# Another order of the VectorE and ScalarE work in the first two chunks of each feed-forward layer

## The chip, the cores and the metric

The kernel runs on one core of a Trainium2 chip. The metric is the device time of one execution in microseconds (us); less is better. The program is written engine by engine: TensorE (PE), VectorE (DVE), ScalarE (ACT), GpSimd (POOL) and the DMA queue of SyncE (SP) each have an instruction list of their own that runs strictly in its order, and semaphores tie the lists together.

## The reference

The input x has 256 tokens of 1024 numbers. Seven stages follow: a hybrid mixer, a feed-forward layer, a convolution block, a second feed-forward layer, a third one that opens the second block, a retention and pooling stage, and a fourth feed-forward layer, with a last norm. The change touches the four feed-forward layers alone. Each is (with a weight of 1 or 0.5 on the last sum)

```python
def swiglu(h, wg, wu, wd):
    return (jax.nn.silu(h @ wg) * (h @ wu)) @ wd

h = h + weight * swiglu(rms_norm(h, gain), wg, wu, wd)      # wg, wu: 1024 x 2816, wd: 2816 x 1024, all float32
```

## The kernel before, in words

**Split products.** Every float32 matmul is three matmuls on rounded parts: an operand is a high part (`whi`, `xh`, `yh`), which ScalarE makes with a rounding copy, and a low part (`wlo`, `xl`, `yl`), which VectorE makes as the value less the high part. `mm3` issues high x high, high x low and low x high (L256, L257, L258).

**Weights as units.** All weights stream through as units of 128 x 2048 numbers (1 MB). There are four raw buffers and four split buffers. `hi(v)` (ACT, L210) waits for unit v to have landed and for the matmuls that used unit v-4 (`used`); `lo(v)` (DVE, L217) waits for `hi(v)`. `hi_half` (ACT, L251) does it in two halves and `lo_quarter` (DVE, L241) in four quarters. SP loads unit v once `lo(v-4)` is done.

**A feed-forward layer** is cut into 11 chunks of 256 hidden columns (j = 0 to 10). Chunk j reads two input units: `quarter` is 12 matmuls (4 k-blocks x 3) of one token half t and one unit, and four quarters make the gate and up columns of the chunk in a PSUM bank per token half. Then

- `scalar_gate_ffn(j, t)` (ACT, L527) takes silu of the gate columns into `sil`,
- `vector_gate_ffn(j, t)` (DVE, L633) multiplies it by the up columns into `hid` and frees the bank. In the layers of weight 0.5 a tiny instruction (L627) scales the norm first, for j = 0,
- `tensor_hidden(j)` (PE, L264) transposes `hid`, both token halves, with four small matmuls.

For chunks 0 to 7 (`FAST` = 8) the product with the down unit is one step of a fast 2 x 2 block scheme with seven products in place of eight. It needs sums of blocks on both sides:

- the activations: `scalar_turned` (ACT) copies the transposed chunk into `turned` (L545) and rounds three of its blocks (L552, signal `turned_hi`); `vector_turned` (DVE, L646) makes their low part; GpSimd forms four sums (L793 to L798); `scalar_sums` (ACT, L556) rounds them, and `vector_sums` (DVE, L651) makes their low part (`sums_lo`),
- the weights: `vector_mix` (DVE, L664 to L670, four instructions) forms the sums of the down unit, one of them in place in the raw buffer, which `hi_half` of that unit must wait for; `scalar_mixed` (ACT, L562) rounds three of them and `vector_mixed` (DVE, L675) makes their low part (`mixed_lo`).

`tensor_fast(j, products)` (PE) issues the named products, three matmuls each. Products 0, 1 and 3 use blocks of `turned`; 2, 4, 5 and 6 use the sums. Products 3, 5 and 6 also need `mixed_lo`.

**Units of a layer.** u0 and u0+1 are the input of chunk 0, u0+2 and u0+3 of chunk 1, u0+4 the down unit of chunk 0, u0+5 and u0+6 the input of chunk 2, u0+7 the down unit of chunk 1.

**PE's order in chunk 1:** quarter (u0+2, t=0); `tensor_hidden(0)`; quarter (u0+3, t=0); products 0 and 1 of chunk 0; quarter (u0+2, t=1), which goes into bank 7 like the t=0 part and so waits for `vector_gate_ffn(1, 0)` to free it; quarter (u0+3, t=1); products 2 and 3; `tensor_hidden(1)`; products 4, 5 and 6. Chunks 2 to 8 repeat this.

**DVE's order in chunks 0 and 1 before:** low parts of the normed activations of t=1 (L361), `lo(u0+3)`, mix 0, gate (0,0), `lo(u0+4)`, gate (0,1), `lo(u0+5)`, turned 0, sums 0, gate (1,0), mixed 0, mix 1, quarters 0 and 1 of u0+6, gate (1,1), quarters 2 and 3 of u0+6.

**ACT's order before:** norm of t=1 (L344, L353), `hi(u0+3)`, gate (0,0), both halves of u0+4, gate (0,1), `hi(u0+5)`, turned 0, sums 0, mixed 0, gate (1,0), `hi(u0+6)`, gate (1,1), first half of u0+7, turned 1, second half of u0+7.

Of the kernel before, what the change touches and what calls it, by code (L numbers as in the profile page):

```python
# [9 lines left out]
FAST = 8  # L10
# [119 lines left out]
def build(nc, xin, wst, wg, wg2, cst, par, brow, cosin, rmask, pmat, dft, w_dw, b_dw, out):  # L130
    NU = wst.shape[0]
    assert NU == sum(UNITS.values())
    with ExitStack() as ctx:
# [3 lines left out]
        sig = Signals(nc, ctx)  # L137
# [95 lines left out]
            if k == n - 1:  # L233
                sig.alias("lo", (v,), "lo_piece", (v, k))

        def lo_quarter(e, q, v, k):
            q.wait_ge(*sig.at("hi", v))
            if v >= S:
                q.wait_ge(*sig.at("used", v - S))
            cols = slice(UC // 4 * k, UC // 4 * k + UC // 4)  # L240
            e.tensor_tensor(wlo[:, v % S, cols], raw[:, v % R, cols], whi[:, v % S, cols].bitcast(F32),  # L241
                            ALU.subtract).then_inc(*sig.up("lo", v) if k == 3 else sig.up("lo_quarter", v, k))
# [58 lines left out]
        def x_of(name):  # L301
            return lambda t, j: banks.emptied("x", name, t, j)
# [172 lines left out]
        def tensor_ffn(e, q, f):  # L475
            units, weight, before, following, _ = FF[f]
            u0 = U[units]
            x = x_of(f)
            for j in range(FC):
                u, key = ff_in(u0, j), f"{f}_in{j}"  # L480
                fast = 1 <= j <= FAST
                d = ff_down(u0, j - 1)
                quarter(e, q, key, u, 0, 0, in_bank(j, 0), xh, xl, x)
                if j == 0:
                    for half in range(2):
                        turn_x(e, q, f, before, 1, half)
                elif j == 1 or j > FAST + 1:
                    tensor_hidden(e, q, f, j - 1)
                quarter(e, q, key, u, 0, 1, in_bank(j, 0), xh, xl, x)
                if fast:  # L490
                    tensor_fast(e, q, f, d, j - 1, (0, 1))
                if f == "ffn0" and j == FC - 1:
                    tensor_prepare(e, q, 0)
                quarter(e, q, key, u, 1, 0, in_bank(j, 1), xh, xl, x)
                if f == "ffn0" and j == FC - 1:
                    tensor_prepare(e, q, 1)
                quarter(e, q, key, u, 1, 1, in_bank(j, 1), xh, xl, x)
                if f == "ffn0" and j == FC - 1:
                    tensor_prepare(e, q, 2)
                if fast:  # L500
                    tensor_fast(e, q, f, d, j - 1, (2, 3))
                    tensor_hidden(e, q, f, j)
                    tensor_fast(e, q, f, d, j - 1, (4, 5, 6))
            sig.alias("x_free", (f,), "full5", (f"{f}_in{FC - 1}", 1))
            u = [ff_down(u0, j) for j in range(FAST, FC)]
            for t in range(2):
                q.wait_ge(*sig.at("yl", f, FAST))
                out_part(e, q, f, u[0], t, 2 * (FAST % 4), yh, yl, ACC[t], first=True)
                if t == 0:
                    tensor_hidden(e, q, f, FC - 1)  # L510
            for n in range(1, 3):
                q.wait_ge(*sig.at("yl", f, FAST + n))
                out_part(e, q, f, u[n], 0, 2 * ((FAST + n) % 4), yh, yl, ACC[0], last=n == 2)
            out_part(e, q, f, u[1], 1, 2 * ((FAST + 1) % 4), yh, yl, ACC[1])
            if following:
                for half in range(2):
                    turn_x(e, q, following, f, 0, half)
            out_part(e, q, f, u[2], 1, 2 * ((FAST + 2) % 4), yh, yl, ACC[1], last=True)
            sig.alias("y_free", (f,), "full3", ("acc", f, 1, 1))
# [44 lines left out]
        def scalar_ffn(e, q, f):  # L564
            units, weight, before, following, _ = FF[f]
            u0 = U[units]
            norm_act(e, q, f, before, 1)
            hi(e, q, u0 + 3)
            scalar_gate_ffn(e, q, f, 0, 0)
            hi_half(e, q, u0 + 4, 0)  # L570
            hi_half(e, q, u0 + 4, 1)
            scalar_gate_ffn(e, q, f, 0, 1)
            hi(e, q, u0 + 5)
            for j in range(1, FAST + 1):
                d = ff_down(u0, j - 1)
                if j == 1:
                    scalar_turned(e, q, f, 0)
                scalar_sums(e, q, f, j - 1)
                if j > 1:
                    hi(e, q, d + 1)  # L580
                scalar_mixed(e, q, f, j - 1)
                scalar_gate_ffn(e, q, f, j, 0)
                hi(e, q, d + 2)
                scalar_gate_ffn(e, q, f, j, 1)
                hi_half(e, q, d + 3, 0)
                if j < FAST:
                    scalar_turned(e, q, f, j)
                else:
                    scalar_hidden(e, q, f, j)
                hi_half(e, q, d + 3, 1)  # L590
            q.wait_ge(*banks.filled("fast", f, 0))
            q.wait_ge(*sig.at("mixed_lo", ff_down(u0, FAST - 1)))
            e.activation(fastw[0], ps[FAST_BANK[0]][:, :], ACT.Copy, bias=0.0, scale=1.0).then_inc(*banks.empty("fast", f, 0))
            hi(e, q, u0 + 29)
            scalar_gate_ffn(e, q, f, FC - 2, 0)
            if f == "ffn0":
                scalar_taps(e, q)
            hi(e, q, u0 + 30)
            scalar_gate_ffn(e, q, f, FC - 2, 1)
            hi(e, q, u0 + 31)  # L600
            scalar_hidden(e, q, f, FC - 2)
            scalar_gate_ffn(e, q, f, FC - 1, 0)
            if f == "ffn0":
                scalar_waves(e, q)
                scalar_prepare(e, q, 0)
            hi(e, q, u0 + 32)
            if f == "ffn0":
                scalar_prepare(e, q, 1)
            scalar_gate_ffn(e, q, f, FC - 1, 1)
            if f == "ffn0":  # L610
                scalar_prepare(e, q, 2)
            hi(e, q, u0 + 33)
            scalar_hidden(e, q, f, FC - 1)
            hi(e, q, u0 + 34)
            if following:
                norm_act(e, q, following, f, 0, sig.at("x_free", f))
            hi(e, q, u0 + 35)
# [112 lines left out]
        def vector_ffn(e, q, f):  # L730
            units, weight, before, following, _ = FF[f]
            u0 = U[units]
            norm_dve(e, q, f, 1)
            lo(e, q, u0 + 3)
            vector_mix(e, q, f, 0)
            vector_gate_ffn(e, q, f, 0, 0)
            lo(e, q, u0 + 4)
            vector_gate_ffn(e, q, f, 0, 1)
            lo(e, q, u0 + 5)
            for j in range(1, FAST + 1):  # L740
                d = ff_down(u0, j - 1)
                if j > 1:
                    lo(e, q, d)
                vector_turned(e, q, f, j - 1)
                vector_sums(e, q, f, j - 1)
                if j > 1:
                    lo(e, q, d + 1)
                vector_gate_ffn(e, q, f, j, 0)
                vector_mixed(e, q, f, j - 1)
                if j < FAST:  # L750
                    vector_mix(e, q, f, j)
                lo_quarter(e, q, d + 2, 0)
                lo_quarter(e, q, d + 2, 1)
                vector_gate_ffn(e, q, f, j, 1)
                lo_quarter(e, q, d + 2, 2)
                lo_quarter(e, q, d + 2, 3)
            vector_hidden(e, q, f, FAST)
            vector_combine(e, q, f, (0,))
            lo(e, q, u0 + 28)
            vector_combine(e, q, f, (1,))  # L760
            vector_gate_ffn(e, q, f, FC - 2, 0)
            lo(e, q, u0 + 29)
            vector_combine(e, q, f, (2,))
            vector_gate_ffn(e, q, f, FC - 2, 1)
            if f == "ffn0":
                vector_taps(e, q)
            lo(e, q, u0 + 30)
            vector_hidden(e, q, f, FC - 2)
            vector_gate_ffn(e, q, f, FC - 1, 0)
            lo(e, q, u0 + 31)  # L770
            if f == "ffn0":
                vector_waves(e, q)
            lo(e, q, u0 + 32)
            vector_gate_ffn(e, q, f, FC - 1, 1)
            lo(e, q, u0 + 33)
            vector_hidden(e, q, f, FC - 1)
            lo(e, q, u0 + 34)
            residual(e, q, f, before, 0, ACC[0], combined=f)
            if following:
                norm_dve(e, q, following, 0)  # L780
            residual(e, q, f, before, 1, ACC[1], combined=f)
            lo(e, q, u0 + 35)
# [1828 lines left out]
```

## Time and profile before

| | |
|---|---|
| median of 3 runs | 1248.78 us (1247.76 to 1249.49) |
| the profiled execution | 1248.3 us |
| its span, first to last instruction | 1246.5 us |
| mean granted TensorE clock | 0.992 of full speed |
| busy: PE, DVE, ACT, POOL | 1207.1, 911.2, 673.1, 100.6 us |
| load of a unit (1 MB), median from issue to landing | 4.8 us |
| starts of the four feed-forward layers (first matmuls of the turned x of t=1) | 149.5, 430.4, 617.0 and 1055.0 us |

All times in rows are from the start of the span. A row of a timeline has a start, a length, the engine, the line, the operation, and out<-in; instructions of one kind that follow each other are merged into one row with their count. What stands in brackets is the time that the engine was idle before it and what released it. An engine's neighbouring instructions overlap by some hundredths of a us at their ends.

### The profile page before, as it was taken

To read this page: it belongs to the slowest core of one execution; us is meant where nothing else is said; L and a number is where in the kernel's file an instruction comes from. 1 tells how busy PE (TensorE), PEld (TensorE's weight loads), DVE (VectorE), ACT (ScalarE), POOL (GpSimd) and SP (SyncE) were. 2 spreads that over 40 slices of the span, in tenths; PEclk is the share of its full clock that TensorE was granted. 3 is DMA by queue.
4 is the path that set the end of the run, shared out by engine and by line. 5 is a ranking of instruction groups with operands and counts; after the bars stand their busy time and mean duration, and the time that the engine had idled before them with its cause. 6 is when DMAs were issued, how large, how long until landed. Compare 5 with 4: busy or idle time off the path is not lost.

```text
span 1246.5 us, 14254 instructions
## 1 busy us (share of the span) xinstructions
PE 1207.1 (97%) x5534; PEld 986.8 (79%) x5534; DVE 911.2 (73%) x1124; ACT 673.1 (54%) x810; POOL 100.6 (8%) x171
## 2 busy tenths in 40 slices
PE   7999999999998989999989999999999999899997
PEld 5776878888887868888878888888888878688885
DVE  6556788888669688887688887656477665788883
ACT  6454656655645656654556654555434544665551
POOL 2300011110020011110011110000000000111100
PEclk9999999999999999999999999999999999999999
DMA  9422455555640545555545555745553444455540
GB/s 344 149 101 80 157 210 189 188 197 203 216 173 34 203 162 189 192 200 180 192 165 188 191 198 179 285 178 180 186 199 135 155 183 156 157 195 202 186 168 34
DMA packets 32326, 220.71 MB, mean 177 GB/s; under 512 B 3729, under 2 KB 4129, under 8 KB 6530
## 3 DMA queue, kind: packets, MB, share of 16 engines
q1 hardware_dynamic: 32258, 219.79, 48.9%
q8 instruction: 44, 0.72, 0.2%
q14 instruction: 24, 0.20, 0.0%
HBM read 218.72 MB, written 1.05 MB: 176 GB/s over the span
## 4 chain that ended last, share of the span: by engine, by line
PE 88%; ACT 4%; DVE 4%; issue 2%; POOL 1%; DMA 0%; SPq 0%; POOLq 0%; DVEq 0%; ACTq 0%
PE ps L256 28%; PE ps L258 27%; PE ps L257 27%; PE ps L261 3%; PE ps L264 3%; DVE wlo L217 1%; ACT xh L344 1%; ACT whi L210 1%; POOL st L377 0%; ACT FS L562 0%; ACT AR L353 0%; ACT whi L251 0%; POOL sums L793 0%; DVE hid L633 0%; DMA pr<-in_par 0%
## 5 line engine op out<-in xcount | busy, mean ns | idle before, releaser
L217 DVE TENSOR_TENSOR wlo<-raw,whi 128x2048 fp32r<-128x2048 f32 x166 | 387.7, 2336 | 154.0 <-ACT whi L210 104.6
L256 PE MATMUL ps<-whi,xh 128*128 128x512 f32 x1120 | 445.7, 398 | 10.1 <-DVE hid L633 6.0
L257 PE MATMUL ps<-wlo,xh 128*128 128x512 f32 x1120 | 439.0, 392 | 0.0
L258 PE MATMUL ps<-whi,xl 128*128 128x512 f32 x1120 | 439.0, 392 | 0.0
L210 ACT CAST whi<-raw 128x2048 fp32r<-128x2048 f32 x163 | 311.7, 1913 | 204.6 <-PE ps L258 203.8
L256 PEld LDWEIGHTS ps<-whi,xh 128*128 128x128 f32 x1120 | 211.8, 189 | 61.0 <-DVE hid L633 7.7
L258 PEld LDWEIGHTS ps<-whi,xl 128*128 128x128 f32 x1120 | 212.0, 189 | 45.9
L257 PEld LDWEIGHTS ps<-wlo,xh 128*128 128x128 f32 x1120 | 212.3, 190 | 41.7
L256 PE MATMUL ps<-whi,yh 128*128 128x512 f32 x352 | 142.5, 405 | 0.9 <-DVE yl L1655 0.6
L258 PE MATMUL ps<-whi,yl 128*128 128x512 f32 x352 | 138.1, 392 | 0.0
L257 PE MATMUL ps<-wlo,yh 128*128 128x512 f32 x352 | 138.0, 392 | 0.0
L241 DVE TENSOR_TENSOR wlo<-raw,whi 128x512 fp32r<-128x512 f32 x132 | 85.1, 686 | 27.2 <-ACT whi L210 27.1
L527 ACT ACTIVATE sil<-ps,st 128x256 f32<-128x256 f32 x88 | 41.9, 476 | 84.1 <-PE ps L258 84.1
L377 POOL TENSOR_TENSOR st<-st,nhalf 128x1 f32<-128x1 f32 (+3 forms) x28 | 28.1, 1002 | 705.6 <-DVE st L368 402.2
L251 ACT CAST whi<-raw 128x1024 fp32r<-128x1024 f32 x72 | 74.8, 1044 | 12.0 <-DVE raw L666 10.1
L256 PEld LDWEIGHTS ps<-whi,yh 128*128 128x128 f32 x352 | 66.7, 189 | 14.8 <-DVE yl L1655 1.0
L258 PEld LDWEIGHTS ps<-whi,yl 128*128 128x128 f32 x352 | 66.6, 189 | 14.2
L257 PEld LDWEIGHTS ps<-wlo,yh 128*128 128x128 f32 x352 | 66.8, 190 | 12.2
L344 ACT ACTIVATE xh<-ps,pr 128x128 fp32r<-128x128 f32 x112 | 30.5, 382 | 51.6 <-PE ps L264 48.3
L675 DVE TENSOR_TENSOR FS<-AR,FS 128x1536 fp32r<-128x1536 f32 x32 | 55.9, 1748 | 0.0
L633 DVE SCALAR_TENSOR_TENSOR hid<-ps,st,sil 128x256 f32<-128x256 f32 x88 | 42.5, 483 | 18.0 <-ACT sil L527 15.4
L793 POOL TENSOR_TENSOR sums<-AR 128x128 f32<-128x128 f32 x32 | 17.0, 530 | 432.6 <-ACT AR L545 432.6
(215 smaller groups left out, 1127.5 us busy)
## 6 DMA issues: line engine op xcount, KB each, us to landing
raw<-in_w SPq DMA_DIRECT2D x199, 1024.0 KB, 4.8
raw<-in_w SPq DMA_DIRECT2D x4, 256.0 KB, 4.9
raw<-in_w SPq DMA_DIRECT2D x2, 512.0 KB, 6.9
AR<-in_b_pw SPq DMA_DIRECT2D x1, 1024.0 KB, 4.8
AR<-in_gate_bias SPq DMA_DIRECT2D x1, 1024.0 KB, 8.5
out<-AR SPq DMA_DIRECT2D x2, 512.0 KB, 2.6
AR<-in_dft SPq DMA_DIRECT2D x1, 864.0 KB, 7.6
AR<-in_rmask SPq DMA_DIRECT2D x1, 768.0 KB, 10.1
```

The source lines that it names most:

```text
L210: e.copy(whi[:, v % S, :], raw[:, v % R, :]).then_inc(*sig.up("hi", v))
L217: e.tensor_tensor(wlo[:, v % S, :], raw[:, v % R, :], whi[:, v % S, :].bitcast(F32), ALU.subtract).then_inc(*sig.up("lo", v))
L241: e.tensor_tensor(wlo[:, v % S, cols], raw[:, v % R, cols], whi[:, v % S, cols].bitcast(F32), ALU.subtract).then_inc(*sig.up("lo", v) if k ...
L251: e.copy(whi[:, v % S, cols], raw[:, v % R, cols]).then_inc(*sig.up("hi", v) if k else sig.up("hi_half", v))
L256: e.matmul(o, ah, bh, start=start, stop=False, skip_group_check=skip)
L257: e.matmul(o, ah, bl, start=False, stop=False, skip_group_check=skip)
L258: return e.matmul(o, al, bh, start=False, stop=stop, skip_group_check=skip)
L261: return e.matmul(o, a, b, start=start, stop=stop, skip_group_check=skip)
L344: last = e.activation(xh[:, k, tcols(t)], ps[b][:, 128 * i:128 * i + 128], ACT.Copy, bias=0.0, scale=parm(name, k))
L527: e.activation(sil[:, t, :], ps[banks.of[key, t]][:, 0:256], ACT.Silu, bias=0.0, scale=rstd[:, t:t + 1]).then_inc(*sig.up("sil", f, j, t))
L633: e.scalar_tensor_tensor(out=hid[:, t, :], in0=ps[b][:, 256:512], scalar=scale, in1=sil[:, t, :], op0=ALU.mult, op1=ALU.mult).then_inc(*ba ...
L675: e.tensor_tensor(mixl, mix, mixh.bitcast(F32), ALU.subtract).then_inc(*sig.up("mixed_lo", v))
```

## The change

In chunks 0 and 1 of every feed-forward layer:

- DVE: mix 0 goes in front of `lo(u0+3)`; gate (0,1) goes in front of the split of u0+4; that of u0+4 and u0+5 is made in quarters, the first two of u0+4 as soon as its first half is rounded; turned 0 and gate (1,0) go between quarters 1 and 2 of u0+5; mixed 0 and mix 1 go in front of sums 0; u0+6 is split whole, behind gate (1,1).
- ACT: gate (0,1) goes in front of the halves of u0+4; gate (1,0) and then mixed 0 go in front of sums 0.
- PE: in all chunks 1 to 8, product 3 is issued in front of product 2.

```diff
-        def lo_quarter(e, q, v, k):
-            q.wait_ge(*sig.at("hi", v))
+        def lo_quarter(e, q, v, k, ready="hi"):
+            q.wait_ge(*sig.at(ready, v))
...
                 if fast:
-                    tensor_fast(e, q, f, d, j - 1, (2, 3))
+                    tensor_fast(e, q, f, d, j - 1, (3, 2))
                     tensor_hidden(e, q, f, j)
                     tensor_fast(e, q, f, d, j - 1, (4, 5, 6))
...
             norm_act(e, q, f, before, 1)
             hi(e, q, u0 + 3)
             scalar_gate_ffn(e, q, f, 0, 0)
+            scalar_gate_ffn(e, q, f, 0, 1)
             hi_half(e, q, u0 + 4, 0)
             hi_half(e, q, u0 + 4, 1)
-            scalar_gate_ffn(e, q, f, 0, 1)
             hi(e, q, u0 + 5)
+            scalar_turned(e, q, f, 0)
             for j in range(1, FAST + 1):
                 d = ff_down(u0, j - 1)
                 if j == 1:
-                    scalar_turned(e, q, f, 0)
-                scalar_sums(e, q, f, j - 1)
-                if j > 1:
+                    scalar_gate_ffn(e, q, f, 1, 0)
+                    scalar_mixed(e, q, f, 0)
+                    scalar_sums(e, q, f, 0)
+                else:
+                    scalar_sums(e, q, f, j - 1)
                     hi(e, q, d + 1)
-                scalar_mixed(e, q, f, j - 1)
-                scalar_gate_ffn(e, q, f, j, 0)
+                    scalar_mixed(e, q, f, j - 1)
+                    scalar_gate_ffn(e, q, f, j, 0)
                 hi(e, q, d + 2)
...
             norm_dve(e, q, f, 1)
+            vector_mix(e, q, f, 0)
             lo(e, q, u0 + 3)
-            vector_mix(e, q, f, 0)
             vector_gate_ffn(e, q, f, 0, 0)
-            lo(e, q, u0 + 4)
             vector_gate_ffn(e, q, f, 0, 1)
-            lo(e, q, u0 + 5)
-            for j in range(1, FAST + 1):
+            for k in range(4):
+                lo_quarter(e, q, u0 + 4, k, "hi_half" if k < 2 else "hi")
+            lo_quarter(e, q, u0 + 5, 0)
+            lo_quarter(e, q, u0 + 5, 1)
+            vector_turned(e, q, f, 0)
+            vector_gate_ffn(e, q, f, 1, 0)
+            lo_quarter(e, q, u0 + 5, 2)
+            lo_quarter(e, q, u0 + 5, 3)
+            vector_mixed(e, q, f, 0)
+            vector_mix(e, q, f, 1)
+            vector_sums(e, q, f, 0)
+            vector_gate_ffn(e, q, f, 1, 1)
+            lo(e, q, u0 + 6)
+            for j in range(2, FAST + 1):
                 d = ff_down(u0, j - 1)
-                if j > 1:
-                    lo(e, q, d)
+                lo(e, q, d)
                 vector_turned(e, q, f, j - 1)
                 vector_sums(e, q, f, j - 1)
-                if j > 1:
-                    lo(e, q, d + 1)
+                lo(e, q, d + 1)
                 vector_gate_ffn(e, q, f, j, 0)
                 vector_mixed(e, q, f, j - 1)
```

## Rows read from the trace of the kernel before

**Rows 1.** Waits of PE: line, releaser, us in total, times, longest.

```profile
PE ps L264 <- DVE hid L633: 9.6, 4, 2.5
```

**Rows 2.** Timeline of PE, first feed-forward layer, chunks 0 to 2.

```profile
158.17 0.39 PE L258 MATMUL ps<-whi,xl 128*128 128x512 f32 x1
...
160.89 0.39 PE L258 MATMUL ps<-whi,xl 128*128 128x512 f32 x1
163.56 0.63 PE L264 MATMUL ps<-kc,hid 128*128 128x128 f32 x4 [2.28 <-DVE hid L633]
...
170.58 0.50 PE L256 MATMUL ps<-whi,xh 128*128 128x512 f32 x1 [0.70 <-DVE hid L633]
...
177.52 0.60 PE L264 MATMUL ps<-kc,hid 128*128 128x128 f32 x4
...
180.02 0.39 PE L256 MATMUL ps<-whi,xh 128*128 128x512 f32 x1
```

**Rows 3.** Timeline of PE, same places of the second and the fourth feed-forward layer.

```profile
444.48 0.62 PE L264 MATMUL ps<-kc,hid 128*128 128x128 f32 x4 [2.28 <-DVE hid L633]
451.51 0.50 PE L256 MATMUL ps<-whi,xh 128*128 128x512 f32 x1 [2.28 <-DVE hid L633]
...
1069.24 0.63 PE L264 MATMUL ps<-kc,hid 128*128 128x128 f32 x4 [2.50 <-DVE hid L633]
1076.28 0.50 PE L256 MATMUL ps<-whi,xh 128*128 128x512 f32 x1 [2.31 <-DVE hid L633]
```

**Rows 4.** Timeline of DVE, first feed-forward layer, chunks 0 to 2.

```profile
154.99 2.29 DVE L217 TENSOR_TENSOR wlo<-raw,whi 128x2048 fp32r<-128x2048 f32 x1 [1.65 <-ACT whi L210]
157.20 0.68 DVE L664 TENSOR_TENSOR AR<-raw 128x512 f32<-128x512 f32 x1
...
160.73 2.29 DVE L217 TENSOR_TENSOR wlo<-raw,whi 128x2048 fp32r<-128x2048 f32 x1 [0.26 <-ACT whi L251]
162.94 0.48 DVE L633 SCALAR_TENSOR_TENSOR hid<-ps,st,sil 128x256 f32<-128x256 f32 x1
...
165.53 0.81 DVE L646 TENSOR_TENSOR yl<-AR,yh 128x384 fp32r<-128x384 f32 x1
...
170.44 1.75 DVE L675 TENSOR_TENSOR FS<-AR,FS 128x1536 fp32r<-128x1536 f32 x1
...
175.64 1.29 DVE L241 TENSOR_TENSOR wlo<-raw,whi 128x512 fp32r<-128x512 f32 x2 [0.47 <-ACT whi L210]
...
182.75 0.55 DVE L646 TENSOR_TENSOR yl<-AR,yh 128x384 fp32r<-128x384 f32 x1
```

**Rows 5.** Timeline of ACT, first feed-forward layer, chunks 0 and 1.

```profile
154.81 0.53 ACT L527 ACTIVATE sil<-ps,st 128x256 f32<-128x256 f32 x1
158.69 2.00 ACT L251 CAST whi<-raw 128x1024 fp32r<-128x1024 f32 x2 [3.36 <-DVE raw L666]
...
160.96 1.89 ACT L210 CAST whi<-raw 128x2048 fp32r<-128x2048 f32 x1
164.22 0.60 ACT L545 ACTIVATE AR<-ps 128x512 f32<-128x512 f32 x1 [1.38 <-PE ps L264]
164.85 0.51 ACT L552 CAST yh<-AR 128x384 fp32r<-128x384 f32 x1
...
168.17 1.48 ACT L562 CAST FS<-AR 128x1536 fp32r<-128x1536 f32 x1
```

**Rows 6.** Timeline of POOL, first feed-forward layer, chunks 0 and 1.

```profile
164.90 1.03 POOL L793 TENSOR_TENSOR sums<-AR 128x128 f32<-128x128 f32 x1 [10.91 <-ACT AR L545]
...
178.83 0.46 POOL L793 TENSOR_TENSOR sums<-AR 128x128 f32<-128x128 f32 x1 [11.22 <-ACT AR L545]
```

**Rows 7.** Windows: stretch, length, busy us (instructions) of each engine, granted clock, DMA share, GB/s.

```profile
163.56:167.62 4.06, 4.06 (x13) 3.28 (x14) 2.78 (x2) 1.11 (x2) 2.63 (x4) 0.58 0.80 295
...
444.40:448.60 4.20, 4.12 (x20) 3.50 (x21) 2.87 (x2) 1.14 (x3) 2.64 (x4) 1.00 0.84 289
```

**Rows 8.** Timeline of SP's queue: the load that follows the split of unit u0.

```profile
133.62 0.33 SPq L2341 DMA_DIRECT2D raw<-in_w  x1
```

## Prediction

> **What bounds the kernel now.** I read the waits of PE first, then the timelines of the engines from the start of the first feed-forward layer, and then the same places of the other three. PE waits rarely, and the largest wait is one of the four feed-forward layers: the transpose of `hid` waits for the gate on VectorE, 9.6 us in four waits [rows 1]. In the first layer PE could go on at 160.89 + 0.23 = 161.12 (12 matmuls take 160.89 - 158.17 = 2.72, so 0.227 each) and goes on at 163.56, 2.44 later. It is held again before quarter (u0+2, t=1), until 170.58, by gate (1,0), which must free bank 7 [rows 2]. From 180.02 on, chunk 2, it runs without a wait. So the reader is to see one stretch per layer, 161.12 to 180.02, 18.90 us long.
>
> What would it take without waits? The transposes cost 2.50 (177.52 to 180.02) less nine matmuls, 0.46 [rows 2]. In the stretch stand 2 x 0.46, 12 + 6 + 24 + 6 = 48 matmuls (10.90) and the last nine (2.04): 13.86. So 5.0 us are there to be had in a layer, and no more.
>
> The half clock is no part of it. In the first layer the granted clock was 0.58 for 4.06 us after the first wait, that is partly 1.2 and partly 2.4 GHz; in the second it was 1.00 in the same place [rows 7]. Yet from the first release to the second took 7.02 us in the one and 7.03 in the other [rows 2, 3]: a chain over ACT, POOL, ACT and DVE sets the second release, and a PE that got there sooner only waited longer (2.28 against 0.70).
>
> **Why the first wait is there.** Gate (0,1) could start when chunk 0 is done: 158.17 + 0.39 = 158.56 and a silu of 0.5 [rows 2, 5]. But ACT first rounds both halves of u0+4, which wait for mix 0 (idle 3.36), and DVE makes `lo(u0+4)`, 160.73 to 163.02, ahead of the gate [rows 4, 5].
>
> **The change, walked through in the first layer.**
>
> DVE: it was idle for 1.65 before `lo(u0+3)`, so from 153.34 [rows 4]. Mix 0 goes there: four instructions of 0.69 and 0.04 between them, 2.9, to 156.24. `lo(u0+3)`, 2.29, ends at 158.53, 1.2 later than before (157.28); PE needs it at 161.6. Gate (0,0) to 158.95.
>
> ACT: silu (0,1) 158.60 to 159.1. Gate (0,1) on DVE ends at 159.6, and PE wants it at 161.12. The first wait goes, with a margin of 1.5.
>
> ACT then makes the halves of u0+4 (2.00, to 161.0) and `hi(u0+5)` (1.89, to 162.8) [rows 5]. The transposes end at about 161.8, so turned 0 is now late by ACT's own queue: 162.8, rounding done 0.6 + 0.5 later, 163.9. This is the new tight place.
>
> DVE meanwhile: u0+4 in quarters, pairs of 1.29 [rows 4], 160.05 to 162.6; quarters 0 and 1 of u0+5, 162.8 to 164.1; turned 0 behind them, 0.55 if undisturbed (second row of its kind), done 164.6. POOL's sums now run beside this. Before, POOL's first sum took 1.03 beside DVE's work and 0.46 without, and turned 0 took 0.81 beside POOL's and 0.55 without [rows 4, 6]. I charge 0.27 twice, for the quarter and for turned 0, as that row is the nearest thing: 165.15. The ends are nothing (164.6) and a whole slow POOL sum of 1.03 (165.65).
>
> The Trainium skill ("SBUF — State Buffer", "Who interferes with whom") says that a VectorE instruction with two inputs in SBUF and a GpSimd instruction that reads SBUF exclude each other, the later one waiting for the end of the earlier. The two rows just named agree with it, and by it VectorE and GpSimd would take turns here, which is the second rival below; the sum does not need it.
>
> PE: 161.12 + 0.46 + 2.72 = 164.30 at products 0 and 1; it waits until 165.15 and its first matmul after a wait is 0.1 longer (0.50 against 0.39, [rows 2]). Six matmuls, 1.36: 166.6. Gate (1,0): its bank is full at 164.5, silu to 164.95, DVE behind turned 0 to 165.6. Bank 7 is free 1.0 before PE asks: the second wait goes. 24 matmuls, 5.45: 172.05.
>
> What is late next: product 3 needs `mixed_lo`. ACT's rounding (1.48, from 164.95) ends at 166.4, DVE after quarters 2 and 3 of u0+5 (167.1) gives it at 168.8. Fine. Mix 1 (2.9) to 171.7, sums 0 (0.69) to 172.4. Product 2 comes at 172.05 + 0.68 = 172.73. In the old order it would come at 172.05 and wait 0.35; that is all that the swap is worth, in chunk 1 alone; in later chunks PE waited for neither, and it costs nothing there. Rounding of the sums on ACT: POOL ends between 165.3 and 167.5 (four of 0.46 to 1.03 from 163.4), so it is done by 168.1 at the latest, before DVE's 171.7. Gate (1,1): silu to 172.7, gate to 173.2; the transposes come at 172.05 + 1.36 = 173.4. As tight as before, but free. `lo(u0+6)`, now whole, ends at 175.5; PE needs it at 178.6.
>
> Chunk 2 then starts at 173.4 + 2.50 = 175.9 in place of 180.02: **4.1 us gained**. It goes on as before, every queue in the same place relative to PE.
>
> Loads: that of u0+4 was issued at 133.6 [rows 8]; at the table's median of 4.8 to landing it is there 15 us before mix 0 wants it. That of u0+7 goes out 1.2 later, 158.6, and is wanted by mix 1 at 168.8. SP's list is not reordered.
>
> The second layer has the same waits to 0.01. In the fourth (and the third, which repeats it) the first wait is 2.50 in place of 2.28, for the small scaling in front of gate (0,1) [rows 3]; the margin of 1.5 covers that, so 4.3. Sum: 2 x 4.1 + 2 x 4.3 = 16.8. The profiled execution took 1248.3; less 16.8 it is 1231.5. The median of the runs is 0.5 above it: **1232.0 us**.
>
> **Rivals.**
>
> 1. POOL and DVE hardly disturb each other: 4.6 a layer, 18.8 in all, 1230; with no wait at all 5.0 and 5.2, 1228.4. Against it: the one place where both ran together shows both lengthened [rows 4, 6]. Chance 0.10.
>
> 2. VectorE becomes the bound. Its work from 153.34 to the end of gate (1,1) adds up to about 17.9 us, to 171.2, against 173.2 in the walk; there is little room. If each instruction beside POOL pays, turned 0 is at 165.65 and sums 0 at 173.0, later than product 2: 0.7 less in a layer, 14.0 in all, 1234.8. Chance 0.14.
>
> 3. The clock falls. The stretch is now PE's own, so a half clock would cost: 4.06 x (1 - 0.58) = 1.7 a layer [rows 7]; in two layers 1235.4, in four 1238.8. Against it: the wait left is 0.85, and the clock fell only after waits of over 2.2, and not after each of them. Chance 0.08.
>
> 4. The other side: mix 0 now heads DVE's list and waits for the load of u0+4 and for the last product of the stage before. Were it held, `lo(u0+3)` and both gates would stand behind it. Up to 1.5 late costs nothing, then 1 for 1 in each layer; 1.5 + 4.1 = 5.6 late, so mix 0 at 159, takes back the whole, and at 6.3 the kernel is slower, about 1251.5. The load would have to take 25 us. Chance 0.03.
>
> 5. The freed time is given back later, by a load or a split that only just came in time: no change, 1248.5. Against it: PE waited for nothing from chunk 2 on, and DVE and ACT hang on PE there and come earlier with it; only loads could lag, and the table's 4.8 us stands against a chunk of some 16. Chance 0.03.
>
> The walk as it stands (1230.5 to 1233.8): 0.62.
>
> **Range.** A change of under 0.2% (2.5 us) can't be told from none. Faster by more: 0.94; within: 0.03; slower: 0.03. The range takes in rival 1 at one end and rivals 2 and most of 3 at the other: 1228.5 to 1237.
>
> **What would show it.** The waits of PE for the gate before the transposes are gone from all four layers, and the wait for bank 7 with them; in their place stands one of 0.4 to 1.4 on turned 0 (L646) before products 0 and 1. Gate (0,1) starts about 2 us ahead of the transposes. Product 2 does not wait. From the first transpose of a layer's `hid` to chunk 2 it is 14.8, where it was 16.5 (163.56 to 180.02), and the transpose comes 2.4 sooner. Wrong I would be if mix 0 starts later than 155, if the clock is under 1 behind the transposes, or if sums 0 ends behind product 3.

## The result and the profile after

The changed kernel takes 1239.53 us, median of 4 runs (1238.23 to 1240.40); the kernel before took 1248.27 beside it (1247.73 to 1249.49). The ratio is 0.9928, interval 0.9911 to 0.9945: faster by 0.7%, 8.7 us. Forecast were 1232.0 us (1228.5 to 1237) and a gain of 16.8. The direction was right; the size was half, and the time lies outside the range.

The profiled execution took 1238.23 us, its span is 1236.4, so 10.1 us shorter than that of before. First PE in the first feed-forward layer (timeline of PE, changed kernel). The lines of PE and ACT have the numbers of before; in the changed kernel the gate on VectorE is L636, turned 0 L649, sums L654, and the sums on POOL L805 to L810, and in runs that add or drop lines above them POOL's are a few off again.

```profile
161.56 0.60 PE L264 MATMUL ps<-kc,hid 128*128 128x128 f32 x4
...
165.67 0.47 PE L256 MATMUL ps<-whi,yh 128*128 128x512 f32 x1 [0.74 <-DVE yl L649]
...
172.59 0.39 PE L256 MATMUL ps<-FS,yh 128*128 128x512 f32 x1
...
173.95 0.60 PE L264 MATMUL ps<-kc,hid 128*128 128x128 f32 x4
...
176.47 0.39 PE L256 MATMUL ps<-whi,xh 128*128 128x512 f32 x1
...
184.85 0.50 PE L256 MATMUL ps<-whi,xh 128*128 128x512 f32 x1 [1.41 <-DVE hid L636]
...
191.79 0.60 PE L264 MATMUL ps<-kc,hid 128*128 128x128 f32 x4
```

PE gets to the transposes 0.4 later than in the trace of before (161.56 and 161.12), for reasons ahead of them. The wait before the transposes [rows 1, 2] is gone, and so is the one for bank 7 in chunk 1. The only wait up to chunk 2 is 0.74 on turned 0. From the first transposes to chunk 2 it is 176.47 - 161.56 = 14.91 (forecast 14.8). But then, in chunk 2, a wait of 1.41 stands at 184.85 that was not there before: again bank 7, again the gate. From the transposes of chunk 1 to those of chunk 2 it takes 191.79 - 173.95 = 17.84. Before, these stood at 177.52 [rows 2] and 193.67, 16.15 apart. Waits of PE over the whole kernel, and the same places of the fourth layer:

```profile
PE ps L256 <- DVE hid L636: 5.7, 4, 1.4
...
PE ps L256 <- DVE yl L649: 3.0, 4, 0.8
...
1063.21 0.47 PE L256 MATMUL ps<-whi,yh 128*128 128x512 f32 x1 [0.76 <-DVE yl L649]
...
1082.37 0.50 PE L256 MATMUL ps<-whi,xh 128*128 128x512 f32 x1 [1.42 <-DVE hid L636]
```

Every layer does the same. Who makes gate (2,0) late? DVE, POOL and ACT of the changed kernel, from the end of chunk 1 on:

```profile
171.99 0.69 DVE L654 TENSOR_TENSOR yl<-sums,yh 128x512 fp32r<-128x512 f32 x1
173.29 0.48 DVE L636 SCALAR_TENSOR_TENSOR hid<-ps,st,sil 128x256 f32<-128x256 f32 x1 [0.61 <-ACT sil L527]
173.69 2.28 DVE L217 TENSOR_TENSOR wlo<-raw,whi 128x2048 fp32r<-128x2048 f32 x1
176.71 2.57 DVE L217 TENSOR_TENSOR wlo<-raw,whi 128x2048 fp32r<-128x2048 f32 x1 [0.74 <-ACT whi L251]
...
182.11 2.29 DVE L217 TENSOR_TENSOR wlo<-raw,whi 128x2048 fp32r<-128x2048 f32 x1 [1.12 <-ACT whi L210]
184.32 0.48 DVE L636 SCALAR_TENSOR_TENSOR hid<-ps,st,sil 128x256 f32<-128x256 f32 x1
```

```profile
175.26 1.04 POOL L805 TENSOR_TENSOR sums<-AR 128x128 f32<-128x128 f32 x1 [8.38 <-ACT AR L545]
...
176.68 0.46 POOL L808 TENSOR_TENSOR sums<-sums,AR 128x128 f32<-128x128 f32 x1
177.22 2.39 POOL L810 TENSOR_TENSOR sums<-AR,sums 128x128 f32<-128x128 f32 x1
```

```profile
179.64 0.62 ACT L556 CAST yh<-sums 128x512 fp32r<-128x512 f32 x1 [2.96 <-POOL sums L810]
180.17 1.91 ACT L210 CAST whi<-raw 128x2048 fp32r<-128x2048 f32 x1
181.98 1.47 ACT L562 CAST FS<-AR 128x1536 fp32r<-128x1536 f32 x1
183.36 0.46 ACT L527 ACTIVATE sil<-ps,st 128x256 f32<-128x256 f32 x1
```

Read it from POOL. Its first sum takes 1.04 in place of 0.46: it starts at 175.26, under the split of u0+6, and ends 0.33 behind that split's end (175.97). So its last sum starts at 177.22, and now the split of u0+7 (176.71 to 179.28) is ahead of it. It ends at 179.61, 0.33 behind that one. A sum of 128 x 128 numbers took 2.39 us. ACT then runs without a gap from 179.64 to 183.8, with the silu of gate (2,0) last in its list. VectorE's split of u0+8, which stands in front of gate (2,0), waits for its rounding (ACT, 180.17 to 182.08) and ends at 184.40; the gate comes behind it, and PE had asked for the bank at 183.3. The kernel before, the same chunks (DVE, POOL, PE):

```profile
163.33 2.28 DVE L217 TENSOR_TENSOR wlo<-raw,whi 128x2048 fp32r<-128x2048 f32 x1
...
180.28 2.54 DVE L217 TENSOR_TENSOR wlo<-raw,whi 128x2048 fp32r<-128x2048 f32 x1 [1.73 <-ACT whi L251]
...
180.22 0.46 POOL L798 TENSOR_TENSOR sums<-AR,sums 128x128 f32<-128x128 f32 x1
...
193.67 0.60 PE L264 MATMUL ps<-kc,hid 128*128 128x128 f32 x4
```

There the last sum started 0.06 ahead of the split: it took 0.46, and the split 2.54 in place of 2.28. Against the transposes of chunk 1 the split has not moved (2.76 behind them before and after); the last sum has, from 2.70 to 3.27. Below, "the lock" is short for this: of a GpSimd sum and a VectorE split that overlap, the one that starts second gets no further until the first has ended.

### The profile page after: what moved, and what is told of

Same layout as the page of the kernel before. It is cut to its first block, busy times and chain, and to the rows that moved or that the text cites. A ratio compares the mean times of both kernels' runs of the same rounds, so it can differ in the third digit from the quotient of the medians.

```text
span 1236.4 us, 14266 instructions
## 1 busy us (share of the span) xinstructions
PE 1201.7 (97%) x5534; PEld 982.5 (79%) x5534; DVE 915.2 (74%) x1136; ACT 672.8 (54%) x810; POOL 113.6 (9%) x171
## 3 DMA queue, kind: packets, MB, share of 16 engines
HBM read 218.72 MB, written 1.05 MB: 178 GB/s over the span
## 4 chain that ended last, share of the span: by engine, by line
PE 88%; ACT 3%; DVE 3%; POOL 2%; issue 2%; DMA 0%; SPq 0%; POOLq 0%; DVEq 0%; ACTq 0%
PE ps L256 28%; PE ps L258 27%; PE ps L257 27%; PE ps L261 3%; PE ps L264 3%; ACT whi L210 2%; POOL st L377 1%; POOL sums L810 1%; ACT whi L251 1%; DVE wlo L217 1%; DMA raw<-in_w 0%; DVE wlo L241 0%; POOL sums L805 0%; DVE yl L649 0%; ACT xh L344 0%
## 5 line engine op out<-in xcount | busy, mean ns | idle before, releaser
L217 DVE TENSOR_TENSOR wlo<-raw,whi 128x2048 fp32r<-128x2048 f32 x162 | 378.6, 2338 | 145.9 <-ACT whi L210 101.0
L241 DVE TENSOR_TENSOR wlo<-raw,whi 128x512 fp32r<-128x512 f32 x148 | 97.2, 700 | 28.1 <-ACT whi L210 26.5
L636 DVE SCALAR_TENSOR_TENSOR hid<-ps,st,sil 128x256 f32<-128x256 f32 x88 | 42.5, 483 | 17.0 <-ACT sil L527 14.9
L805 POOL TENSOR_TENSOR sums<-AR 128x128 f32<-128x128 f32 x32 | 17.1, 535 | 409.5 <-ACT AR L545 409.5
```

The lines of the kernel that those rows point to most:

```text
L217: e.tensor_tensor(wlo[:, v % S, :], raw[:, v % R, :], whi[:, v % S, :].bitcast(F32), ALU.subtract).then_inc(*sig.up("lo", v))
L636: e.scalar_tensor_tensor(out=hid[:, t, :], in0=ps[b][:, 256:512], scalar=scale, in1=sil[:, t, :], op0=ALU.mult, op1=ALU.mult).then_inc(*ba ...
```

## The experiments

Each kernel was timed beside the kernel before. Twelve ran.

**A wait added.** The changed kernel, where VectorE waits for POOL's last sum before the split of u0+7:

```diff
                 d = ff_down(u0, j - 1)
+                if j == 2:
+                    q.wait_ge(*sig.at("sums", f, 1))
                 lo(e, q, d)
```

> The changed kernel with one wait more: in chunk 2 VectorE starts the split of u0+7 only when GpSimd has made the last of its sums of chunk 1. In the changed kernel that split (176.71 to 179.28) ran over the last sum, which took 2.39 us in place of 0.46, and PE waited 1.41 for gate (2,0). Theory 1 (VectorE's two-input instructions shut GpSimd out until they end): the split starts 1.0 later, but the sums are there at about 177.7 in place of 179.6; the last sum takes under 1 us, PE's wait in chunk 2 falls from 1.4 to 0.4 to 0.5 in each layer, and the kernel is 3 to 4 us faster than the changed one, though a wait was added. Theory 2 (VectorE has simply run out of time, since the split of u0+6 now stands behind gate (1,1)): the added wait makes gate (2,0) about 1 later, PE's wait grows to 2.4, and the kernel is 4 us slower than the changed one.

1233.77 us (1233.15 to 1234.63), ratio 0.9876 (0.9861 to 0.9890): some 6 us faster than the changed kernel, by a wait. POOL's last sum, DVE and PE:

```profile
176.66 0.46 POOL L812 TENSOR_TENSOR sums<-AR,sums 128x128 f32<-128x128 f32 x1
...
177.16 2.29 DVE L217 TENSOR_TENSOR wlo<-raw,whi 128x2048 fp32r<-128x2048 f32 x1 [1.73 <-POOL sums L812]
...
183.17 0.50 PE L256 MATMUL ps<-whi,xh 128*128 128x512 f32 x1 [0.29 <-DVE hid L636]
```

The sum takes 0.46 again, PE's wait is 0.29. Theory 2 (VectorE has run out of time) said 4 us slower and is out. The gain is above the 3 to 4 expected. PE's wait shrank by 1.1 a layer, 4.5 in all, and not by 0.9 to 1.0; the spans of the two profiled executions differ by 5.0, and the rest is within the spread of the runs.

**The split of u0+7 in quarters**, same place, same wait for its rounding:

```diff
-                lo(e, q, d)
+                if j == 2:
+                    for k in range(4):
+                        lo_quarter(e, q, d, k)
+                else:
+                    lo(e, q, d)
```

> The changed kernel with the split of u0+7 in chunk 2 cut into four quarters, in the same place and with the same wait for its rounding. VectorE does 0.2 us more. Theory 1 (GpSimd is shut out to the end of the running VectorE instruction): the last sum slips in behind the first quarter and takes at most 1.0 us; the sums are there by 177.8; PE's wait of 1.41 before quarter (u0+5, t=1) is gone, and the kernel is 5.5 to 6.8 us faster than the changed one. Theory 2 (VectorE is out of time): gate (2,0) comes 0.2 later and the kernel is 0 to 1 us slower than the changed one.

1232.72 us (1232.38 to 1235.28), ratio 0.9874 (0.9857 to 0.9890); once more beside other kernels 1234.99 (1232.64 to 1235.36), 0.9891 (0.9877 to 0.9906). POOL's last sum slips in behind the first quarter:

```profile
176.27 3.05 DVE L241 TENSOR_TENSOR wlo<-raw,whi 128x512 fp32r<-128x512 f32 x4 [0.74 <-ACT whi L251]
...
176.78 0.79 POOL L814 TENSOR_TENSOR sums<-AR,sums 128x128 f32<-128x128 f32 x1
...
173.50 0.60 PE L264 MATMUL ps<-kc,hid 128*128 128x128 f32 x4
...
189.98 0.60 PE L264 MATMUL ps<-kc,hid 128*128 128x128 f32 x4
```

PE's wait for the gate is gone from the list of its waits, and chunk 2 takes 16.48, where it took 17.84, and 16.15 in the kernel before. The gain of 6.8 is at the upper end of what was expected; by the ratio of the second series (0.9891, where the changed kernel had 0.9928) it is some 4.6. VectorE does more work here than in the changed kernel (four quarters took 2.50 where one split takes 2.28). This version beats both kernels.

**The same lock set off in the kernel before**, by 0.46 us more on the least busy engine:

```diff
                 e.tensor_tensor(s3, a11, a21, ALU.subtract).then_inc(*sig.up("sum3", f, j))
+                q.wait_ge(*sig.at("sum3", f, j))
+                e.tensor_tensor(s3, a11, a21, ALU.subtract).then_inc(*sig.up("sum3_again", f, j))
```

> The kernel before with 0.46 us more work on GpSimd, the least busy engine: its second sum is made twice in every chunk. In the trace of before the last sum started at 180.22 and VectorE's split of the next down unit at 180.28, so it was 0.06 ahead. Lock theory: now the split is ahead by 0.4, the last sum waits for its end and takes some 2.2 us, the rounding of the sums and all behind it on ScalarE are 1.9 later, and PE waits 1.2 to 1.4 for the gate in each of chunks 2 to 8 of each layer: 28 x 1.3, 30 to 40 us slower. Without a lock: the sums come 0.5 later, the silu had 1.14 of idle time in front of it, so no difference in chunks 2 to 8, and at most 0.5 a layer in chunk 1: 0 to 2 us slower.

1299.02 us (1297.57 to 1301.57), ratio 1.0411 (1.0395 to 1.0426): 51 us slower. The split of u0+7, the last sum, PE in chunk 2, and PE's waits over the kernel:

```profile
181.29 2.54 DVE L217 TENSOR_TENSOR wlo<-raw,whi 128x2048 fp32r<-128x2048 f32 x1 [1.74 <-ACT whi L251]
...
181.77 2.39 POOL L800 TENSOR_TENSOR sums<-AR,sums 128x128 f32<-128x128 f32 x1
...
189.40 0.50 PE L256 MATMUL ps<-whi,xh 128*128 128x512 f32 x1 [1.38 <-DVE hid L633]
...
PE ps L256 <- DVE hid L633: 47.3, 32, 2.8
```

Once in each of the 28 chunks from the second on, as the lock theory has it, PE waits for the gate; the four waits left are those for bank 7 in chunk 1. The size was put too low: a chunk takes 196.38 - 178.53 = 17.85 in place of 16.15, so 1.7 and not 1.3, and 28 x 1.7 = 48. It is the same 1.7 that the change lost in its one chunk a layer. The rest is in chunk 1, which is 0.5 to 0.6 longer in three layers and 2.2 in the remaining one.

**Parts undone.** First, on both engines, sums 0 in front of gate (1,0) again (ScalarE: sums, mixed, silu):

```diff
-                    scalar_gate_ffn(e, q, f, 1, 0)
-                    scalar_mixed(e, q, f, 0)
                     scalar_sums(e, q, f, 0)
+                    scalar_mixed(e, q, f, 0)
+                    scalar_gate_ffn(e, q, f, 1, 0)
...
             vector_turned(e, q, f, 0)
-            vector_gate_ffn(e, q, f, 1, 0)
             lo_quarter(e, q, u0 + 5, 2)
             lo_quarter(e, q, u0 + 5, 3)
+            vector_sums(e, q, f, 0)
+            vector_gate_ffn(e, q, f, 1, 0)
             vector_mixed(e, q, f, 0)
             vector_mix(e, q, f, 1)
-            vector_sums(e, q, f, 0)
```

> The changed kernel with the old order around sums 0: ScalarE rounds sums 0, then mixed 0, then makes silu (1,0); VectorE makes sums 0 in front of gate (1,0), mixed 0 and mix 1. From the changed trace: sums rounded to 167.5, mixed 0 to 168.9, silu to 169.3, gate (1,0) to 169.8, where PE asks for bank 7 at 167.1. The prediction's account (the second wait is the chain over sums and mixed that stands in front of the gate): a wait of 2.7 comes back in every layer, 10 to 11 us slower than the changed kernel, about 1250. If the second wait was only the tail of the first: under 2 us slower.

1255.60 us (1253.97 to 1256.09), ratio 1.0053 (1.0038 to 1.0068): slower than the kernel before, and 15.5 slower than the changed one, not 10 to 11. The wait is there, but it takes more than itself along (PE, then two windows; the last columns are the granted clock, the DMA share and GB/s):

```profile
160.98 0.60 PE L264 MATMUL ps<-kc,hid 128*128 128x128 f32 x4
...
169.09 0.80 PE L256 MATMUL ps<-whi,xh 128*128 128x512 f32 x1 [2.40 <-DVE hid L636]
...
177.63 0.60 PE L264 MATMUL ps<-kc,hid 128*128 128x128 f32 x4
```

```profile
164.00:168.00 4.00, 1.96 (x8) 1.05 (x6) 3.36 (x5) 1.85 (x2) 2.04 (x3) 1.00 0.97 354
168.00:172.00 4.00, 2.91 (x7) 2.33 (x8) 3.31 (x4) 0.52 (x2) 0.00 (x0) 0.64 1.00 387
```

Behind the wait TensorE ran at 1.2 GHz for part of the next four us. From the wait to the transposes of chunk 1 it took 8.54; in the kernel before, with the same matmuls at the full clock, 177.52 - 170.58 = 6.94. That is 1.6, and the other layers show it too: chunk 1 takes 16.50 to 16.65 in all four, 4.1 to 4.3 more than in the changed kernel. The wait for the gate in chunk 2 (1.4 in each layer) stays.

**Gate (0,1) first, alone**, on the kernel before:

```diff
             scalar_gate_ffn(e, q, f, 0, 0)
+            scalar_gate_ffn(e, q, f, 0, 1)
             hi_half(e, q, u0 + 4, 0)
             hi_half(e, q, u0 + 4, 1)
-            scalar_gate_ffn(e, q, f, 0, 1)
...
-            lo(e, q, u0 + 4)
             vector_gate_ffn(e, q, f, 0, 1)
+            lo(e, q, u0 + 4)
```

> The kernel before with one part alone: gate (0,1) in front of the rounding of u0+4 on ScalarE and in front of its split on VectorE. The wait of 2.3 to 2.5 before the transposes goes (gate done at about 160.9, PE there at 161.1). But the split of u0+5 still stands before turned 0, and sums 0 and mixed 0 before the silu of gate (1,0), so PE waits some 2 us before products 0 and 1 or before bank 7. Expected: 1.0 to 2.0 a layer gained over the kernel before, 4 to 8 in all. If the first wait alone had been the cost: 2.4 a layer, 9.6.

1249.73 us over ten runs (1246.50 to 1255.40), ratio 1.0010 (0.9995 to 1.0025): no gain, where 4 to 8 us were expected. The profiled execution was the slowest of them:

```profile
167.41 0.47 PE L256 MATMUL ps<-whi,yh 128*128 128x512 f32 x1 [1.89 <-DVE yl L646]
...
171.50 0.79 PE L256 MATMUL ps<-whi,xh 128*128 128x512 f32 x1 [1.66 <-DVE hid L633]
...
164.38 2.46 POOL L793 TENSOR_TENSOR sums<-AR 128x128 f32<-128x128 f32 x1 [9.34 <-ACT AR L545]
```

The first wait is gone and others stand in its place: PE waits 7.5 us for turned 0 and 8.1 for the gate, 15.6 in all, and before it was 9.6 and 6.0, also 15.6. The second release was hardly moved: it comes 171.50 - 162.17 = 9.33 behind the first transposes, and before it came 170.58 - 161.12 = 9.46 behind the moment at which PE could have made them. Here too POOL's first sum is shut out, 2.46 us, by the split of u0+5, which started 0.13 ahead of it. In three of the four layers the half clock came behind these waits (0.50 from 169 to 173 in the first), and chunk 1 took 17.6 to 17.9; in the fourth it did not, and chunk 1 took 16.0. By and large the clock goes with the time: the run at a mean of 0.997 took 1246.50, the one at 0.988 took 1255.40.

**Mix 0 behind the split of u0+3 again:**

```diff
-            vector_mix(e, q, f, 0)
             lo(e, q, u0 + 3)
+            vector_mix(e, q, f, 0)
```

> The changed kernel with mix 0 behind the split of u0+3 again. The 1.65 us that VectorE sits idle there before is not used. Gate (0,1) ends at about 161.4 against 161.56 when PE wants it, so the first wait does not come back; all of VectorE's work behind is later by up to 1.2, and PE's wait before products 0 and 1 grows from 0.74 to between 1.0 and 1.9. 1 to 3.5 us slower than the changed kernel. If VectorE has slack there: no difference.

1241.50 us (1240.11 to 1242.20), ratio 0.9941 (0.9926 to 0.9956), beside 1240.05 (1238.05 to 1240.68) for the changed kernel run again. 1.4 slower, too little for these runs to tell, at the low end of the expectation. The wait before products 0 and 1 grew as expected in two layers only (1.48 and 1.50); in the other two it was 0.60 and 0.65 (4.2 in all, where the changed kernel has 3.0).

> The changed kernel once more, beside the others on one chip: 1238 to 1241 us, PE's wait of 1.4 in chunk 2 of every layer. Half-clock stretches between the layers, which come in some executions and not in others, spread the runs by 2 us.

So it was: 1240.05, ratio 0.9928 (0.9913 to 0.9943), 5.7 us of waits for the gate, 1.4 each.

**The swap of products 2 and 3**, undone in the changed kernel, and undone in the version with quarters, each by

```diff
-                    tensor_fast(e, q, f, d, j - 1, (3, 2))
+                    tensor_fast(e, q, f, d, j - 1, (2, 3))
```

> The changed kernel with product 2 in front of product 3 again. The low part of the sums was ready at 172.68 in the changed kernel, where PE got to these products at 172.59. From this trace: a wait of 0.1 to 0.2 in chunk 1 of each layer, 0.4 to 0.8 in all, so no difference that can be told. The prediction's walk had 0.35 a layer, 1.4 in all. If the swap matters elsewhere (last chunk), over 2 us.

> The changed kernel with the split of u0+7 in quarters and product 2 in front of product 3 again. Now no later wait in chunk 2 can hide what the swap is worth. Low part of sums 0 ready 0.1 behind the moment at which PE gets there: 0.1 to 0.2 a layer, 0.4 to 0.8 us slower than with product 3 first; the prediction's walk: 0.35 a layer, 1.4 us.

1241.11 us (1240.19 to 1242.46), ratio 0.9935 (0.9920 to 0.9950), and 1234.12 (1233.16 to 1236.33), ratio 0.9894 (0.9878 to 0.9911), against 0.9928 and 0.9891: no difference in either. The traces say why. Transposes of chunks 1 and 2, with 2 first (fence one) and with 3 first (fence two), both in quarters:

```profile
161.18 0.60 PE L264 MATMUL ps<-kc,hid 128*128 128x128 f32 x4
...
173.87 0.60 PE L264 MATMUL ps<-kc,hid 128*128 128x128 f32 x4
...
190.07 0.60 PE L264 MATMUL ps<-kc,hid 128*128 128x128 f32 x4
```

```profile
161.50 0.60 PE L264 MATMUL ps<-kc,hid 128*128 128x128 f32 x4
...
173.89 0.60 PE L264 MATMUL ps<-kc,hid 128*128 128x128 f32 x4
...
190.38 0.60 PE L264 MATMUL ps<-kc,hid 128*128 128x128 f32 x4
```

Chunk 1 takes 12.69 against 12.39: the swap brings 0.30, near the 0.35 of the walk and more than the 0.1 to 0.2 expected. Chunk 2 takes 16.20 against 16.49 and gives it back; to the end of chunk 2 both take 28.88 to 28.89. In the changed kernel it is the same (12.66 + 17.57 and 12.39 + 17.84, both 30.23). What holds chunk 2 did not move with the swap: in the first layer of all four traces VectorE's split of u0+6 starts 12.13 to 12.14 behind the first transposes, and POOL's first sum, shut out by it, ends 14.74 behind them.

**Two further versions**, both from the one with quarters. In the first, turned 0 and mixed 0 go in front of u0+5 on both engines:

```diff
-            hi(e, q, u0 + 5)
             scalar_turned(e, q, f, 0)
...
-                    scalar_gate_ffn(e, q, f, 1, 0)
                     scalar_mixed(e, q, f, 0)
+                    scalar_gate_ffn(e, q, f, 1, 0)
+                    hi(e, q, u0 + 5)
                     scalar_sums(e, q, f, 0)
...
-            lo_quarter(e, q, u0 + 5, 0)
-            lo_quarter(e, q, u0 + 5, 1)
             vector_turned(e, q, f, 0)
+            vector_mixed(e, q, f, 0)
             vector_gate_ffn(e, q, f, 1, 0)
-            lo_quarter(e, q, u0 + 5, 2)
-            lo_quarter(e, q, u0 + 5, 3)
-            vector_mixed(e, q, f, 0)
             vector_mix(e, q, f, 1)
             vector_sums(e, q, f, 0)
+            for k in range(3):
+                lo_quarter(e, q, u0 + 5, k)
             vector_gate_ffn(e, q, f, 1, 1)
+            lo_quarter(e, q, u0 + 5, 3)
```

> A further version: the changed kernel with the split of u0+7 in quarters, and turned 0 and mixed 0 in front of the rounding and the split of u0+5 on both engines, gate (1,0) behind mixed 0, then mix 1, sums 0, three quarters of u0+5, gate (1,1), the last quarter. Turned 0 is ready at 163.8 and no longer holds products 0 and 1; mixed 0 holds gate (1,0) for about 0.4 and gate (1,1) may come 0.3 late. If it goes so: 0 to 0.5 a layer less than with the quarters alone, 1231 to 1233. If VectorE's work is the bound whatever its order: no gain over the quarters alone, or a loss of 1 to 2 us.

1240.42 us (1237.93 to 1241.44), ratio 0.9930 (0.9912 to 0.9948): the gain of the quarters is lost, more than either branch of the expectation allowed. PE waits 0.80 for gate (1,0) in chunk 1 in place of the 0.74 on turned 0, so chunk 1 is no shorter (12.49); chunk 2 takes 17.73. The last quarter of u0+5 pushes the split of u0+6 over POOL's first sum, and it starts the same slide:

```profile
174.65 1.64 POOL L808 TENSOR_TENSOR sums<-AR 128x128 f32<-128x128 f32 x1 [10.34 <-ACT AR L545]
...
178.10 0.79 POOL L813 TENSOR_TENSOR sums<-AR,sums 128x128 f32<-128x128 f32 x1
```

In the second, only quarter 1 of u0+5 moves behind gate (1,0):

```diff
-            lo_quarter(e, q, u0 + 5, 1)
             vector_turned(e, q, f, 0)
             vector_gate_ffn(e, q, f, 1, 0)
+            lo_quarter(e, q, u0 + 5, 1)
```

> A further version: the changed kernel with the split of u0+7 in quarters, and quarter 1 of u0+5 moved behind gate (1,0), so that one quarter and not two stands in front of turned 0. Turned 0 was rounded at 164.23 in the changed kernel and its low part started at 164.71: it can start 0.4 sooner, and PE's wait of 0.74 before products 0 and 1 falls to 0.3. If VectorE's work behind it still comes in time: 1.6 us less than with the quarters alone, about 1231. If sums 0 or gate (1,1) are pushed too late: the same or up to 1 us more.

> The changed kernel with the split of u0+7 in quarters, once more, beside the two others: 1232 to 1234 us.

1233.64 us (1232.39 to 1233.74), ratio 0.9882 (0.9868 to 0.9897), against 0.9891 (0.9877 to 0.9906): the medians differ by 1.35 us, and the two can't be told apart by times. PE's wait on turned 0 fell to 0.30 as expected. The transposes of chunk 1 came only 0.09 sooner behind those of chunk 0 (173.54 - 161.24 = 12.30, and 12.39 above), because product 2 waits now:

```profile
163.95 0.81 DVE L649 TENSOR_TENSOR yl<-AR,yh 128x384 fp32r<-128x384 f32 x1 [0.34 <-ACT yh L552]
165.16 0.48 DVE L636 SCALAR_TENSOR_TENSOR hid<-ps,st,sil 128x256 f32<-128x256 f32 x1 [0.40 <-ACT sil L527]
...
172.00 0.68 DVE L654 TENSOR_TENSOR yl<-sums,yh 128x512 fp32r<-128x512 f32 x1
...
172.74 0.50 PE L256 MATMUL ps<-whi,yh 128*128 128x512 f32 x1
```

VectorE stood idle for 0.34 and 0.40 on the way and ended sums 0 at 172.68, 11.44 behind the first transposes, where with the quarters alone it was 11.12. But the trace shows 0.3 more in chunk 2: gate (1,1) and the split of u0+6 start 0.4 sooner, and that chunk takes 16.19 in place of 16.49. To the end of chunk 2 it is 28.49 in place of 28.88 in the first layer, and 28.50 to 28.51 in place of 28.88 to 28.90 in the others: the 0.4 a layer that was expected, too little to be shown by these runs' times.

## Why the prediction was half right

**Right, to 0.2 us, up to the start of chunk 2.** The first wait went. The wait on turned 0 was 0.74 (walk: 0.85), the second wait is gone, product 3 went ahead without one, the transposes of chunk 1 came 12.39 behind the first ones (walk: 173.4 - 161.12 = 12.28). The gain to the start of chunk 2 was 2.44 + 16.46 - 14.91 = 3.99 where the walk had 4.1. The account of the clock held too: no layer of the profiled changed kernel shows a half-clock stretch behind the transposes. One reading was loose, without effect on the sum: the second layer has the same first wait and the same 7.03 between the releases, but its second wait is 2.28 and not 0.70 [rows 2, 3].

**The step that failed** is "It goes on as before, every queue in the same place relative to PE", and with it the pricing of the split of u0+6, which was moved whole behind gate (1,1): "`lo(u0+6)`, now whole, ends at 175.5; PE needs it at 178.6". It ended at 175.97 (14.41 behind the first transposes; walk: 14.38), and PE had it in time. But it was priced against PE alone. GpSimd's first sum starts under it; the sum's end moves by 0.58, the last sum falls behind the start of the split of u0+7, which stands still relative to PE, and waits for its end. Chunk 2 takes 1.69 more in each layer (17.84 against 16.15).

**The account.** Two layers at 3.99, two at about 4.3 as forecast (the first wait of 2.50, by the walk's count 2.66, and 1.62 between the transposes of chunks 0 and 1, 13.98 before and 12.36 after: 4.28): 16.5, where 16.8 was forecast. Less 4 x 1.69 = 6.8: 9.8. The spans differ by 10.1. The medians differ by 8.7: the profiled execution of the changed kernel was its fastest, and its runs lie in two pairs, 1238.2 and 1238.8 at a mean clock of 0.997, 1240.3 and 1240.4 at 0.992. In the changed kernel's second series the profiled run has the clock at 0.90 of full speed from 1020 to 1024 and at 0.68 from 1024 to 1028, ahead of the fourth layer, where the first series' profile has 1.00. That such stretches make up the whole spread is not shown.

**The rule was at hand.** The Trainium skill ("SBUF — State Buffer", "Who interferes with whom") was cited for exactly this: the later of the two waits for the end of the earlier. The traces agree: the last sum, started under a split, took 2.39 us in place of 0.46. I priced it at 0.27 for an instruction, from the two rows at hand, and only in chunk 1. The price is what is left of VectorE's instruction, and for the last sum here it came to 1.93. The 1.03 of [rows 6] was already that: the sum started at 164.90, 0.71 before the end of the split of u0+5 (163.33 + 2.28 = 165.61), and ended 0.32 behind it. The trace of before held the warning too: last sum and split 0.06 us apart. Rival 2 named the right resource in the wrong chunk (14.0 gained, 1234.8), and as a matter of VectorE's time; that VectorE had time is shown by the added wait. Rival 5 (the freed time is given back later, chance 0.03) came nearest: 6.8 of 16.5 were given back in chunk 2. I looked there only at loads and splits, not at the GpSimd sums beside them.

**Rival 3** (the clock) did not decide here; that its 1238.8 lies near the measured time is chance. But it is real: with the second wait put back, the half clock cost 1.6 a layer, close to its 1.7. "The half clock is no part of it" held for the kernel before, where PE waited for the chain anyway, and only there. And "the clock fell only after waits of over 2.2" did not last: with gate (0,1) first alone it fell to 0.50 behind a wait of 1.89.

## What to carry to other kernels

Where VectorE and GpSimd both work on data in SBUF, list GpSimd's instructions beside VectorE's long ones with their start times. If a short GpSimd instruction on a chain starts within a few tenths of a long VectorE one, every reordering must be walked through for who comes first, in the chunk after the reordered ones too; here, cutting the long instruction or letting it wait for the short one took PE's 1.4 us of waiting down to 0.3 or less. When a move is priced by "the consumer needs it at", ask also who is shut out while it runs. And compare two traces by distances from a common event, not by times from the start of the span: from trace to trace the first transposes of these kernels lie anywhere from 160.85 to 162.43.

## What the runs showed of the hardware

- A GpSimd sum of 128 x 128 numbers took 0.46 us alone and up to 2.62 when it ran into a VectorE instruction with two SBUF inputs. Such a sum ended 0.31 to 0.33 behind the end of that instruction (175.97 and 176.30, 179.28 and 179.61, and all others of over 0.85 us in the traces of all runs). The other way round, a VectorE split of 2.28 to 2.29 took up to 2.58, the longer the sooner it started behind the sum. The length of the VectorE instruction is thus the price for GpSimd, and the rest of GpSimd's 0.46 the price for VectorE. A longer GpSimd instruction costs it more: a split at 29.51 in the kernel before, 0.06 behind one of 1.05 us, took 3.13.
- Who comes first is a matter of hundredths: all splits that started 0.03 to 0.12 us behind a sum went second, and the sum took under 0.48; the one that started 0.02 behind a sum (third layer, gate (0,1) first alone) took 2.29, and the sum 2.62.
- 0.46 us of GpSimd work more in each chunk, 15 us in all (32 x 0.46) on an engine that is 8% busy, made the kernel 51 us slower.
- The same wait of PE (2.28 us, kernel before) was followed by 1.2 GHz in the first layer and not in the second; ten runs of one kernel spread from 1246.5 to 1255.4 us with the mean granted clock from 0.997 to 0.988.
